# A third unit's split weights in places of their own, and the first feed-forward's pair in two other banks

## The chip, the cores and the metric

The kernel runs on one core of one Trainium2 chip. The metric is the device time of one execution in microseconds, the median of several executions. A trace of one further execution, with every instruction of every engine, was taken with the hardware profiler.

## What is computed

Two transformer-like blocks one behind the other, on one sequence of 512 tokens with 1024 features, all in float32:

```
x = first_block(x, c, ...)     # adaptive shift and scale from c; three mixers (S5, latent attention, gated spatial unit)
                               # merged by gates; layer norm; SwiGLU feed-forward; layer norm
h = second_block(x, ...)       # h += attention(rms(h)); h += swiglu(rms(h)); h += mlstm(rms(h)); h += swiglu(rms(h)); rms(h)

def swiglu(h, w_in, w_out):
    a, b = jnp.split(h @ w_in, 2, axis=-1)      # 1024 x 5632, hidden width 2816
    return (jax.nn.silu(a) * b) @ w_out
```

The attention of the second block has 8 heads in three groups of dilated windows (projection 1024 x 9216, output 1024 x 1024). The mLSTM has 8 heads (projection 1024 x 3088, output 1024 x 1024). There are three feed-forwards: number 0 in the first block, 1 and 2 in the second.

## The kernel before

Activations lie with the 128 features of a tile on the partitions and the 512 tokens along the free dimension; there are KD = 8 such tiles. Almost all of the time goes into multiplying them by weights that are used once. The weights are cut into units of 128 output columns (8 blocks of 128 x 128, and 11 in the feed-forwards' output). Each product is made in three matmuls so that it keeps float32 precision: activations are kept as a high and a low part (h_hi, h_lo), and so are the weights (w_hi, w_lo).

**The path of a unit.** SyncE loads it from memory into one of four raw tiles (N_RAW = 4). GpSimd splits it into w_hi (a pass that adds zero and rounds) and w_lo (a pass that subtracts), in `split_unit` and, inside loops, `split_at`; these go to one of two pairs of places (N_SPLIT = 2), by the unit's number modulo 2. TensorE uses them in `cols_mm` (24 matmuls of 512 columns for a unit of 8 blocks) or, tile by tile, in `tile_mm`. The semaphores count units: `units_split` up to where GpSimd is, `units_used` up to where TensorE is. GpSimd splits unit u only when unit u - 2 is used:

```
wait(pool, "units_used", u - N_SPLIT + 1)
```

All engines work through their instructions in order, and the order is written out by hand. The stages with their unit names are: w_mix_out, w_ff0_in_a, w_ff0_out_a, w_ff0_in_b, w_ff0_out_b, w_att (8 heads of 8 units), w_att_out, then the second feed-forward, w_ml, w_ml_out, and the third feed-forward. A feed-forward is done in two halves, a and b, of FFH = 11 hidden tiles with two units each: the gate and the other factor.

**The start of a stage.** The first two units of a stage are often worked on together (`pair_mm`, order `by_tile`), tile by tile, since the tiles of h_hi and h_lo come one after another from the norm in front of it. Both units are then in use up to the end, and unit 2 of the stage (the third) needs the place of unit 0. In the output projections of the attention and the mLSTM, units 0 and 1 are run over the finished heads while the last head is still being worked on (`last_head`, `last_heads`), and end with the last head's tile.

**First feed-forward.** The pair goes to the two banks g[0] and g[1]. ScalarE makes the tiles of h_hi (`norm_tiles`), then eight tiles of x, the residual (scaled and shifted from xn), then issues a DMA for the positions, and then enters the loop `one`: Silu of the gate bank to ff_s. VectorE multiplies it by the other bank and splits the product into u_hi and u_lo (`hidden`). TensorE's gate of the next hidden tile goes to the same bank, so it waits for the Silu (`gate_free`).

**Attention input.** The first head has its own order (`first_head`): the pair, then units 2 to 5 in the banks bc, ba, bb, bd. Behind unit 3 TensorE sums the rows of squares (`sum_rows`), for which VectorE adds up eight tiles of squares (`add_square`); ScalarE and VectorE make the inverse deviation of it (rstd), and VectorE scales the projections with it. TensorE's value projection (`project_values`) waits for the copies of five of them.

**Residual.** In an output projection VectorE adds each result to x (`tile`), and TensorE reuses a bank when the addition out of it is counted in `res_added`. The next stage's h_hi and h_lo and the squares are made in between.

Memory: the arena of 115 KB is shared by stage; `at(kb, ...)` places a tile at an offset in it. u_hi and u_lo lie at 0 and 22 KB, qk of the even heads at 44 KB, ml_qk at 0 KB.

Of the kernel before, what the change touches and what calls it, by code (L numbers as in the profile page):

```python
# [106 lines left out]
CONV_AT = [1] + [2 * n for n in range(1, 8)]  # L107
CONSTS = 2
# [22 lines left out]
def two_blocks(nc, t, out):  # L131

    ctx = ExitStack()
    with ctx:
# [112 lines left out]
        xn = at(46, "xn", [P, KD, SEQ])  # L247

# [192 lines left out]
        def _(pool):  # L441
# [23 lines left out]

            def low_part(u):
# [36 lines left out]
            for name, size, count in RUNS:  # L503
                u0 = FIRST[name]
                if name == "w_att":
                    with pool.Fori(0, 8) as h:
                        for s in range(8):
                            split_at(8 if s < 6 else 12, h, 8, u0 + s)
                    continue
                n = count // N_RAW  # L510
                if n > 1:
                    with pool.Fori(0, n) as i:
                        for s in range(N_RAW):
                            split_at(size, i, N_RAW, u0 + s)
# [7 lines left out]
        def _(pe):  # L522
# [96 lines left out]
            def residual(name, kb, xs, nth, shift=False, lead=None, **first):  # L619
# [5 lines left out]
                def pair(i):  # L625
                    for s in range(2):
                        ready(i * 2 + (u0 + s))
                        wait(pe, "res_added", i * 2 + (nth * 8 + s - 1))
                        cols_mm(g[(u0 + s) % 2], (u0 + s) % 2, kb, xs, **(first if isinstance(i, int) and s == 0 else {}))
                    if shift and isinstance(i, int):  # L630
                        first_tile()
                if lead is not None:
                    lead()
                    with pe.Fori(1, 4) as i:
# [4 lines left out]
            def feed_forward(n):  # L639
                for half, ab in enumerate("ab"):  # L640
# [17 lines left out]
                    else:  # L658
                        pe.wait_ge(S["res_added"], added - (n > 0))
                        pair_mm((bc, bd) if n else (first, second), u0, (h_hi, h_lo), H_SPLIT[f"ff{n}"] - 8,  # L660
                                late_tile if n else by_tile)
                        if n:
                            sum_rows(SQ[f"ff{n}"])
                            ready(u0 + 2)
                            cols_mm(first, u0 % 2, 8, (h_hi, h_lo))
                            ready(u0 + 3)
                            cols_mm(second, (u0 + 1) % 2, 8, (h_hi, h_lo))
                        with pe.Fori(2 if n else 1, FFH) as i:
# [327 lines left out]
            def first_head(s):  # L996
# [6 lines left out]
                cols_mm((bc, ba, bb, bd)[s - 2], (u0 + s) % 2, 8, (h_hi, h_lo))  # L1003
# [230 lines left out]
        def _(act):  # L1234
# [255 lines left out]
            def feed_forward(n):  # L1490
                for half, ab in enumerate("ab"):
                    u0 = FIRST[f"w_ff{n}_in_{ab}"]
                    j0 = (n * 2 + half) * FFH
                    def one(i):
                        wait(act, "units_used", i * 2 + (u0 + 1))
                        wait(act, "ff_mul", i + j0)
                        act.activation(ff_s[:], g[u0 % 2], ACT.Silu).then_inc(S["ff_silu"], 1)  # L1497
# [5 lines left out]
                    if n == 0:  # L1503
                        peeled(act, FFH, one)
                        if half == 0:
                            wait(act, "pos_phase", 1)
                            act.activation(rope_s[:], a0, ACT.Sin)
                            act.activation(rope_c[:], a1, ACT.Sin)
                            act.drain().then_inc(S["pos_trig"], 1)
                        continue  # L1510
# [6 lines left out]
            for k in range(KD):  # L1517
                act.activation(x[:, k, :], xn[:, k, :], ACT.Identity, scale=ln_cols[:, 2, k:k + 1], bias=ln_cols[:, 3, k:k + 1])
            act.drain()
# [1171 lines left out]
```

## Time and profile before

| | |
|---|---|
| median of 3 runs | 2638.06 us (2636.12 to 2644.28) |
| the profiled execution's own time | 2635.93 us |
| its span, first to last instruction | 2634.1 us |
| matmuls | 2481.6 us, 94% of the span |
| VectorE busy | 1489.8 us, 57% |
| GpSimd busy | 1647.6 us, 63% |
| ScalarE busy | 499.8 us, 19% |
| mean granted clock of TensorE | 0.962 of full speed |

A matmul's time in the trace includes its way through the array, and matmuls overlap; the step from one to the next is shorter than the duration shown. Times of day in the rows are microseconds from the span's start.

### The profile page before, as it was taken

The numbers are of one execution on the slowest core, as the hardware profiler recorded it, in microseconds if no ns is written. First come the engines' busy times: TensorE is split into PE (matmuls) and PEld (weight loads), VectorE is DVE, ScalarE is ACT, GpSimd is POOL, SyncE is SP. The second block draws the span as 40 slices with busy tenths as digits, with TensorE's granted clock in tenths as the row PEclk, the third lists the DMA queues.
The fourth block names the chain that finished last, engine by engine and source line by source line (L and its number), as shares of the span: only waits on it lengthen the run. The fifth ranks groups of instructions, "written<-read, shape, count | busy, mean of one in ns | idle before, by whom it ended". The sixth has DMA issues, their size and how long they took to land.

```text
span 2634.1 us, 33940 instructions
## 1 busy us (share of the span) xinstructions
PE 2481.6 (94%) x11937; PEld 2010.8 (76%) x11937; DVE 1489.8 (57%) x1796; ACT 499.8 (19%) x968; POOL 1647.6 (63%) x700
## 2 busy tenths in 40 slices
PE   6998999997999997999999989999999998999997
PEld 4776776775888875888888878888877666888886
DVE  5867334686464467754544455534588567544446
ACT  4533222103000004121211121000141442100000
POOL 4425445574777774655666557777777324787774
PEclk7999999997999998999999999999999989999998
DMA  6212333421332322222222223323322101332331
GB/s 244 71 55 81 123 149 121 152 77 53 96 104 88 102 90 68 77 76 84 77 84 78 81 61 96 113 78 96 112 74 88 48 27 51 92 107 84 96 107 53
DMA packets 61230, 237.70 MB, mean 90 GB/s; under 512 B 7072, under 2 KB 12200, under 8 KB 57424
## 3 DMA queue, kind: packets, MB, share of 16 engines
q1 hardware_dynamic: 54720, 230.51, 26.6%
q10 hardware_dynamic: 6416, 5.95, 0.7%
q8 instruction: 57, 0.93, 0.2%
q14 instruction: 37, 0.30, 0.0%
HBM read 232.24 MB, written 2.10 MB: 89 GB/s over the span
## 4 chain that ended last, share of the span: by engine, by line
PE 83%; DVE 8%; ACT 3%; issue 2%; DVEq 1%; ACTq 1%; POOL 1%; DMA 1%; POOLq 0%
PE gg L532 19%; PE gg L533 19%; PE gg L534 19%; PE babcd L570 2%; PE babcd L572 2%; PE babcd L571 2%; PE gg L906 2%; PE gg L908 1%; PE gg L907 1%; PE babcd L532 1%; PE babcd L533 1%; PE babcd L534 1%; PE babcd L1151 1%; PE be L882 1%; PE be L1177 1%
## 5 line engine op out<-in xcount | busy, mean ns | idle before, releaser
L462 POOL TENSOR_TENSOR w_hi<-raw,zero 128x1024 fp32r<-128x1024 f32 (+2 forms) x280 | 580.9, 2075 | 609.5 <-PE gg L534 386.0
L464 POOL TENSOR_TENSOR w_lo<-raw,w_hi 128x1024 fp32r<-128x1024 f32 (+2 forms) x280 | 748.5, 2673 | 39.9
L532 PE MATMUL gg<-h_hi,w_hi 128*128 128x512 f32 x1568 | 622.6, 397 | 14.4 <-ACT ff_s L1497 5.2
L533 PE MATMUL gg<-h_lo,w_hi 128*128 128x512 f32 x1568 | 617.4, 394 | 0.0
L534 PE MATMUL gg<-h_hi,w_lo 128*128 128x512 f32 x1568 | 616.6, 393 | 0.0
L532 PEld LDWEIGHTS gg<-h_hi,w_hi 128*128 128x128 f32 x1568 | 299.0, 191 | 85.5 <-issue 12.3
L534 PEld LDWEIGHTS gg<-h_hi,w_lo 128*128 128x128 f32 x1568 | 298.5, 190 | 63.4
L533 PEld LDWEIGHTS gg<-h_lo,w_hi 128*128 128x128 f32 x1568 | 298.9, 191 | 60.9
L2027 DVE TENSOR_TENSOR ta<-ff_s,gg 128x512 f32<-128x512 f32 x64 | 44.0, 688 | 331.1 <-PE gg L534 323.6
L453 POOL TENSOR_TENSOR w_hi<-raw,zero 128x1536 fp32r<-128x1536 f32 (+2 forms) x48 | 107.2, 2234 | 188.1 <-PE babcd L534 142.1
L532 PE MATMUL gg<-u_hi,w_hi 128*128 128x512 f32 x528 | 209.7, 397 | 4.2 <-issue 4.2
L533 PE MATMUL gg<-u_lo,w_hi 128*128 128x512 f32 x528 | 208.8, 395 | 0.0
L534 PE MATMUL gg<-u_hi,w_lo 128*128 128x512 f32 x528 | 208.8, 395 | 0.0
L1684 DVE TENSOR_TENSOR u_lo<-ta,u_hi 128x512 f32 (+1 forms) x66 | 178.5, 2704 | 9.3 <-issue 6.0
L455 POOL TENSOR_TENSOR w_lo<-raw,w_hi 128x1536 fp32r<-128x1536 f32 (+2 forms) x48 | 139.1, 2897 | 6.8
L570 PE MATMUL babcd<-w_hi,h_hi 128*128 128x384 f32 (+1 forms) x352 | 127.9, 363 | 9.3 <-ACT pt_res L1567 6.6
L1502 ACT ACTIVATE ff_s<-sq 128x512 f32<-128x512 f32 x44 | 27.9, 634 | 542.8 <-DVEq L2023 539.8
L571 PE MATMUL babcd<-w_hi,h_lo 128*128 128x384 f32 (+1 forms) x352 | 125.7, 357 | 0.0
L572 PE MATMUL babcd<-w_lo,h_hi 128*128 128x384 f32 (+1 forms) x352 | 125.7, 357 | 0.0
L532 PEld LDWEIGHTS gg<-u_hi,w_hi 128*128 128x128 f32 x528 | 99.2, 188 | 30.4 <-issue 6.8
L534 PEld LDWEIGHTS gg<-u_hi,w_lo 128*128 128x128 f32 x528 | 99.2, 188 | 24.0
L533 PEld LDWEIGHTS gg<-u_lo,w_hi 128*128 128x128 f32 x528 | 99.2, 188 | 24.0 <-issue 0.2
(568 smaller groups left out, 3893.0 us busy)
## 6 DMA issues: line engine op xcount, KB each, us to landing
raw<-in_w_ff_in_a SPq DMA_DIRECT2D x66, 512.0 KB, 3.5
raw<-in_w_ff_in_b SPq DMA_DIRECT2D x66, 512.0 KB, 3.5
raw<-in_w_att_qk SPq DMA_DIRECT2D x48, 512.0 KB, 3.6
raw<-in_w_ff_out_a SPq DMA_DIRECT2D x24, 704.0 KB, 4.1
raw<-in_w_ff_out_b SPq DMA_DIRECT2D x24, 704.0 KB, 4.1
late_raw<-in_w_ada SPq DMA_DIRECT2D x16, 1024.0 KB, 5.0
raw<-in_w_ml SPq DMA_DIRECT2D x25, 512.0 KB, 3.5
raw<-in_w_merge_a SPq DMA_DIRECT2D x16, 768.0 KB, 5.3
```

The source lines that it names most:

```text
L453: pool.tensor_tensor(hi, a, zero[:].to_broadcast([P, size * P]), ALU.add)
L455: pool.tensor_tensor(lo, a, hi, ALU.subtract).then_inc(S["units_split"], 1)
L462: pool.tensor_tensor(hi, a, zero[:].to_broadcast([P, size * P]), ALU.add)
L464: pool.tensor_tensor(lo, a, hi, ALU.subtract).then_inc(S["units_split"], 1)
L532: pe.matmul(dst, w_hi[slot][:, blk], xs[0][:, k, :], start=k == 0, stop=False)
L533: pe.matmul(dst, w_hi[slot][:, blk], xs[1][:, k, :], start=False, stop=False)
L534: mm = pe.matmul(dst, w_lo[slot][:, blk], xs[0][:, k, :], start=False, stop=k == kb - 1)
L570: pe.matmul(dst, xs[0][:, k, tok], w_hi[slot][:, blk], start=first and j == 0, stop=False)
L571: pe.matmul(dst, xs[1][:, k, tok], w_hi[slot][:, blk], start=False, stop=False)
L572: mm = pe.matmul(dst, xs[0][:, k, tok], w_lo[slot][:, blk], start=False, stop=last and j == len(ks) - 1)
L906: pe.matmul(g[m % 2], w_hi[slot][:, blk], h_hi[:, k, :], start=k == 0, stop=False)
L1684: v.tensor_tensor(lo, src, hi, ALU.subtract)
```

## The change

Unit 2 of four stages (w_ff0_in_a, w_att, w_att_out, w_ml_out) gets a pair of places of its own in the arena, `w_hi[2..5]` and `w_lo[2..5]`, found by `THIRD[name]`. GpSimd splits it with `split_third`, which waits not for a unit's use but for the former tenant of the place: the last unit of the stage before, or the scores of heads that lie there. TensorE reads it from there. The order of the splits and of the units stays. The loops of GpSimd and TensorE begin one round later, since the first is written out.

In the first feed-forward, half a, the pair goes to the banks bc and bd; units 2 and 3 go to g[0] and g[1], written out before the loop. Silu and `hidden` of the first hidden tile read bc and bd. The eight residual tiles and the DMA of the positions move on ScalarE from in front of the first Silu to behind it.

```diff
+THIRD = {"w_ff0_in_a": 2, "w_att": 3, "w_att_out": 4, "w_ml_out": 5}
...
+        for name, (hi_at, lo_at) in (("w_ff0_in_a", (18, 40)), ("w_att", (0, 4)), ("w_att_out", (44, 48)), ("w_ml_out", (0, 8))):
+            w_hi.append(at(hi_at, f"third_hi_{name}", [P, KD * P], F32R))
+            w_lo.append(at(lo_at, f"third_lo_{name}", [P, KD * P], F32R))
...
+            def split_third(name, tenant, done):
+
+                u, w = FIRST[name] + 2, THIRD[name]
+                pool.wait_ge(S[f"raw_landed{u % N_RAW}"], (u // N_RAW + 1) * 16)
+                pool.wait_ge(S[tenant], done)
+                a, hi, lo = raw[u % N_RAW][:, 0:KD * P], w_hi[w][:], w_lo[w][:]
+                pool.tensor_tensor(hi, a, zero[:, 0:1].to_broadcast([P, KD * P]), ALU.add)
+                pool.drain()
+                pool.tensor_tensor(lo, a, hi, ALU.subtract).then_inc(S["units_split"], 1)
...
+                if name in THIRD:
+                    for s in range(per):
+                        if s == 2:
+                            if name in ("w_ff0_in_a", "w_att"):
+                                split_third(name, "units_used", u0)
+                            elif name == "w_att_out":
+                                split_third(name, "att_scores", 14)
+                            else:
+                                split_third(name, "ml_scores", 4)
+                        else:
+                            split_unit(8 if s < 6 else 12, u0 + s, (u0 + s) % N_RAW, (u0 + s) % N_SPLIT)
...
-                        pair_mm((bc, bd) if n else (first, second), u0, (h_hi, h_lo), H_SPLIT[f"ff{n}"] - 8,
-                                late_tile if n else by_tile)
+                        pair_mm((bc, bd), u0, (h_hi, h_lo), H_SPLIT[f"ff{n}"] - 8, late_tile if n else by_tile)
                         if n:
                             sum_rows(SQ[f"ff{n}"])
-                            ready(u0 + 2)
-                            cols_mm(first, u0 % 2, 8, (h_hi, h_lo))
-                            ready(u0 + 3)
-                            cols_mm(second, (u0 + 1) % 2, 8, (h_hi, h_lo))
-                        with pe.Fori(2 if n else 1, FFH) as i:
+                        ready(u0 + 2)
+                        cols_mm(first, u0 % 2 if n else THIRD["w_ff0_in_a"], 8, (h_hi, h_lo))
+                        ready(u0 + 3)
+                        cols_mm(second, (u0 + 1) % 2, 8, (h_hi, h_lo))
+                        with pe.Fori(2, FFH) as i:
                             gate_up(i)
...
-                cols_mm((bc, ba, bb, bd)[s - 2], (u0 + s) % 2, 8, (h_hi, h_lo))
+                cols_mm((bc, ba, bb, bd)[s - 2], THIRD["w_att"] if s == 2 else (u0 + s) % 2, 8, (h_hi, h_lo))
...
                         if half == 0:
+                            one(0, bank=bc)
+                            for k in range(KD):
+                                act.activation(x[:, k, :], xn[:, k, :], ACT.Identity, scale=ln_cols[:, 2, k:k + 1], bias=ln_cols[:, 3, k:k + 1])
+                            act.drain()
+                            act.dma_start(pos_i[:], t["pos"].partition_broadcast(32)).then_inc(S["att_consts"], 16)
+                            with act.Fori(1, FFH) as i:
+                                one(i)
...
             norm_tiles(0, "ff0", xn)
-            for k in range(KD):
-                act.activation(x[:, k, :], xn[:, k, :], ACT.Identity, scale=ln_cols[:, 2, k:k + 1], bias=ln_cols[:, 3, k:k + 1])
-            act.drain()
-            act.dma_start(pos_i[:], t["pos"].partition_broadcast(32)).then_inc(S["att_consts"], 16)
             feed_forward(0)
```

In `residual`, the stages with a `lead` write out pair 1 (units 2 and 3), whose first unit reads `THIRD[name]`, and loop from 2.

## Rows read from the trace of the kernel before

**Rows 1.** The page: busy times, and the chain that ended last by engine.

```profile
PE 2481.6 (94%) x11937; PEld 2010.8 (76%) x11937; DVE 1489.8 (57%) x1796; ACT 499.8 (19%) x968; POOL 1647.6 (63%) x700
...
PE 83%; DVE 8%; ACT 3%; issue 2%; DVEq 1%; ACTq 1%; POOL 1%; DMA 1%; POOLq 0%
```

**Rows 2.** Two lines of VectorE: durations in ns (min/median/max), first and last start.

```profile
L2027 DVE TENSOR_TENSOR ta<-ff_s,gg x9: 686/687/690, 664.7 to 751.8; 128x512 f32<-128x512 f32 x9
...
L1966 DVE SCALAR_TENSOR_TENSOR x<-gg,one_col,x x6: 750/752/752, 1552.2 to 1580.2; 128x512 f32<-128x512 f32 x6
```

**Rows 3.** Timeline, first feed-forward: start, us, operation [idle before, its releaser].

```profile
607.85 2.08 PE L605 MATMUL bf<-ta,ones 128*128 128x512 f32 x2 [5.51 <-DVEq L1997]
...
632.42 5.75 ACT L1518 ACTIVATE x<-xn,ln_cols 128x512 f32<-128x512 f32 x8
...
634.89 1.89 POOL L462 TENSOR_TENSOR w_hi<-raw,zero 128x1024 fp32r<-128x1024 f32 x1 [27.78 <-PE gg L546]
...
636.93 2.35 POOL L464 TENSOR_TENSOR w_lo<-raw,w_hi 128x1024 fp32r<-128x1024 f32 x1
...
639.89 0.60 ACT L1497 ACTIVATE ff_s<-gg 128x512 f32<-128x512 f32 x1
...
640.63 0.76 PE L532 MATMUL gg<-h_hi,w_hi 128*128 128x512 f32 x1 [5.20 <-ACT ff_s L1497]
```

**Rows 4.** Attention input: the additions of squares together, then the timeline.

```profile
L1934 DVE TENSOR_TENSOR tb<-tb,sq x7: 691/2180/2692, 1031.5 to 1043.5; 128x512 f32<-128x512 f32 x7
...
1033.43 0.63 PE L532 MATMUL babcd<-h_hi,w_hi 128*128 128x512 f32 x1 [3.89 <-POOL w_lo L464]
...
1041.16 4.99 DVE L1934 TENSOR_TENSOR tb<-tb,sq 128x512 f32<-128x512 f32 x2 [0.51 <-ACT sq L1533]
...
1046.24 1.13 PE L592 MATMUL be<-tb,ones 128*128 128x512 f32 x2
...
1061.76 0.69 PE L570 MATMUL babcd<-w_hi,h_hi 128*128 128x384 f32 x1 [2.67 <-DVE qk L2300]
```

**Rows 5.** Timeline, start of the attention's output projection.

```profile
1539.09 0.75 DVE L1966 SCALAR_TENSOR_TENSOR x<-gg,one_col,x 128x512 f32<-128x512 f32 x1 [1.15 <-PE gg L546]
...
1543.98 0.79 PE L532 MATMUL gg<-o_hi,w_hi 128*128 128x512 f32 x1 [4.23 <-POOL w_lo L464]
...
1552.18 0.75 DVE L1966 SCALAR_TENSOR_TENSOR x<-gg,one_col,x 128x512 f32<-128x512 f32 x1 [5.75 <-PE gg L534]
```

**Rows 6.** Timeline, the mLSTM's last head and the start of its output projection.

```profile
2184.59 2.62 POOL L464 TENSOR_TENSOR w_lo<-raw,w_hi 128x1024 fp32r<-128x1024 f32 x1
2186.57 1.19 DVE L2509 SCALAR_TENSOR_TENSOR whole<-og,whole 128x512 f32<-128x512 f32 x1
...
2190.22 0.69 DVE L1704 TENSOR_TENSOR ta<-ta,em 128x512 f32<-128x512 f32 x1
...
2195.98 0.50 PE L544 MATMUL gg<-hd_hi,w_hi 128*128 128x512 f32 x1 [3.10 <-DVE hd_lo L2514]
...
2206.97 0.75 DVE L1966 SCALAR_TENSOR_TENSOR x<-gg,one_col,x 128x512 f32<-128x512 f32 x1 [1.05 <-PE gg L546]
...
2211.86 0.79 PE L532 MATMUL gg<-hd_hi,w_hi 128*128 128x512 f32 x1 [4.23 <-POOL w_lo L464]
...
2220.56 0.75 DVE L1966 SCALAR_TENSOR_TENSOR x<-gg,one_col,x 128x512 f32<-128x512 f32 x1 [6.25 <-PE gg L534]
```

**Rows 7.** Windows: busy us (instructions) of each engine, then granted clock, DMA share, GB/s.

```profile
640.60:644.50 3.90, 3.87 (x9) 3.12 (x10) 3.73 (x3) 0.00 (x0) 2.90 (x2) 0.50 0.33 126
...
1033.40:1037.10 3.70, 3.67 (x9) 2.88 (x10) 3.46 (x3) 2.33 (x5) 3.56 (x2) 0.54 0.58 213
...
1061.80:1067.60 5.80, 5.80 (x18) 5.80 (x19) 5.28 (x9) 0.00 (x0) 3.75 (x2) 0.50 0.17 52
...
2196.00:2199.00 3.00, 3.00 (x14) 2.45 (x14) 1.28 (x2) 0.63 (x1) 0.00 (x0) 1.00 0.02 5
```

**Rows 8.** Idle time ahead of L532's matmuls, 1586 to 1700, by releaser: us, times.

```profile
  POOL w_lo L464: 0.5, 1
```

More of the change, by code:

```diff
@@ L504, in _ @@
                 u0 = FIRST[name]
+                per = 8 if name == "w_att" else N_RAW
+                if name in THIRD:
[9 more added lines that the diff above has]
+                            split_unit(8 if s < 6 else 12, u0 + s, (u0 + s) % N_RAW, (u0 + s) % N_SPLIT)
                 if name == "w_att":
-                    with pool.Fori(0, 8) as h:
+                    with pool.Fori(1, 8) as h:
                         for s in range(8):
@@ L511, in _ @@
                 if n > 1:
-                    with pool.Fori(0, n) as i:
+                    with pool.Fori(int(name in THIRD), n) as i:
                         for s in range(N_RAW):
@@ L628, in pair @@
                         wait(pe, "res_added", i * 2 + (nth * 8 + s - 1))
-                        cols_mm(g[(u0 + s) % 2], (u0 + s) % 2, kb, xs, **(first if isinstance(i, int) and s == 0 else {}))
+                        third = lead is not None and isinstance(i, int) and s == 0
+                        cols_mm(g[(u0 + s) % 2], THIRD[name] if third else (u0 + s) % 2, kb, xs, **(first if isinstance(i, int) and s == 0 else {}))
                     if shift and isinstance(i, int):
@@ L633, in residual @@
                     lead()
-                    with pe.Fori(1, 4) as i:
+                    pair(1)
+                    with pe.Fori(2, 4) as i:
                         pair(i)
@@ L1493, in feed_forward, with one @@
                     j0 = (n * 2 + half) * FFH
-                    def one(i):
+                    def one(i, bank=g[u0 % 2]):
                         wait(act, "units_used", i * 2 + (u0 + 1))
                         wait(act, "ff_mul", i + j0)
-                        act.activation(ff_s[:], g[u0 % 2], ACT.Silu).then_inc(S["ff_silu"], 1)
+                        act.activation(ff_s[:], bank, ACT.Silu).then_inc(S["ff_silu"], 1)
                     def scaled(i):
@@ L1509, in feed_forward @@
                             act.drain().then_inc(S["pos_trig"], 1)
+                        else:
+                            peeled(act, FFH, one)
                         continue
@@ L2033, in scaled_hidden @@
                         hidden(i)
-                    if n == 0:
+                    if n == 0 and half == 0:
+                        hidden(0, bank=bd)
+                        with v.Fori(1, FFH) as i:
+                            hidden(i)
+                    elif n == 0:
                         peeled(v, FFH, hidden)
```

1 line of the change is left out of this document (removed).

## Prediction

> **What bounds the kernel now.** The page comes first: TensorE's matmuls cover 94% of the span and 83% of the chain that ended last, GpSimd is busy 63% and VectorE 57% [rows 1]. So only what stands between two matmuls, or makes matmuls slow, is worth anything. The list of what TensorE waited for shows where it stands still; at each of these places the timeline gives the wait, and the view of windows the clock that was granted behind it. In steady work a weight unit (24 matmuls) takes 5.44 us in the feed-forward inputs (nine products 87.1 us apart over eight pairs of units: 87.1 / 16) and 5.60 us in the output projections (28.0 / 5) [rows 2]. GpSimd needs 1.89 + 2.35 us for its two passes over a unit, up to 2.62 us for the second where VectorE works beside it [rows 3, 6], so it keeps pace. It falls behind only at a stage's start, where units 0 and 1 finish almost together and the split of unit 2 could not begin before.
>
> Four such places are touched. Each early split waits for the former tenant of its place, and every later split stands behind it on GpSimd, which works in order; the tenants (the last unit of the stage before, seven heads' scores, four heads' scores) are done long before GpSimd gets there, so this wait costs nothing. First feed-forward: TensorE idles 5.20 us up to 640.63; here the split was done at 639.28, and the release is the Silu at 639.89, behind the eight residual tiles (5.75 us) [rows 3]. Attention input: 3.89 us up to 1033.43 [rows 4]. Attention output: 4.23 us up to 1543.98 [rows 5]. mLSTM output: a gap of the same kind up to 2211.86 [rows 6]. Behind these gaps the clock is 0.50 to 0.54, the lower of its two levels (1.2 GHz), for about 4 to 6 us; a matmul then takes 3.9 / 9 = 0.43 us instead of 5.44 / 24 = 0.227 [rows 2, 7].
>
> **First feed-forward.** After the change the pair goes to two other banks, so unit 2 needs neither the Silu nor the residual tiles; its split can run from 607 on, while GpSimd had nothing to do for 27.78 us [rows 3]. TensorE leaves the pair at 640.63 - 5.20 = 635.43 and goes on. Unit 3 is split from about 635.5 to 640.2 (1.89 + 0.15 + 2.62); TensorE wants it at 635.43 + 5.44 = 640.87, so the wait is nothing, with only 0.7 us to spare. Units 2 to 5 then end at 635.43 + 4 x 5.44 = 657.2, and the product that read the last of them at 664.7 [rows 2] starts at 657.3: 7.4 us won (5.2 of gap, the rest matmuls at the lower clock). The moved work: the table load and Silu end about 636.7, the eight tiles take 5.75 us, the position DMA's issue about 0.4, so ScalarE is at the second Silu near 643 and done by 644. TensorE asks for it with unit 4, at 646.3; 2 us of cover. Were that gone, each us of ScalarE would cost one.
>
> **Attention output.** Unit 2 is now released by the first residual addition (1539.09 + 0.75 = 1539.84, matmul about 1540.0) and ends at 1545.6; the addition behind it moves from 1552.18 to 1545.7 [rows 5]. 6.5 us won. Its early split follows unit 1's directly, beside the last head's scores, which VectorE reads from PSUM; at worst it holds up a tiny product by 0.5 us, under matmuls. I take nothing. The first additions shift against GpSimd's passes; a unit later they are back in step, since TensorE needs tile k's addition only at unit k + 2; I take nothing and keep 1 us for the range.
>
> **mLSTM output.** The same sum: first addition done 2206.97 + 0.75 = 2207.72, unit 2 from 2207.9 to 2213.5, next addition at 2213.6 instead of 2220.56: 7.0 us [rows 6]. But the early split starts when GpSimd is free, at 2184.59 + 2.62 = 2187.2, and its second pass lasts from about 2189.25 to 2191.6. In that time falls VectorE's maximum of two SBUF tiles at 2190.22 (0.69 us alone), on the chain to the last head's output. Rows tell what such a meeting does: the product of two SBUF tiles at 2186.57 took 1.19 us, ending 0.55 after GpSimd's pass (2187.21) [rows 6]; the sums of two SBUF tiles took 0.69 us alone, and 2.18 at the median, 2.69 at most, beside it [rows 4]. So the maximum ends at 2192.15 rather than 2190.91: 1.24 us lost, between 0 (no meeting) and 2. This lengthens TensorE's idle stretch before 2195.98 from 3.10 to 4.34 us. Behind 3.10 the clock was still 1.00; behind 3.89 and 4.23 it was down [rows 4, 5, 6, 7]. 4.34 lies beyond those, so I take the lower clock for the 12 matmuls ahead of the last square sums: 12 x 0.20 = 2.4 us more lost (0 is the other end). Net 7.0 - 1.2 - 2.4 = 3.4 us, between 3.4 and 7.0.
>
> The Trainium skill, page "SBUF — State Buffer", section "Who interferes with whom", says that a VectorE operation with two SBUF inputs and a GpSimd operation that reads SBUF take one shared port pair in turn, the later one standing still until the first is done. By it the early splits are not free although GpSimd was idle; 2190.22 would be held, as the rows at 2186.57 bear out. Without the rule and its rows the sum would be 3.6 us better here.
>
> **Attention input.** Unit 2 would run from 1029.54 to 1035.0 and unit 3 to 1040.4 instead of 1046, 5.7 us earlier. What is late next is the column-sum of squares behind unit 3: it waits for VectorE's last addition, which ended at 1041.16 + 4.99 = 1046.15, and the matmul came at 1046.24 [rows 4]. Until now the two were level. VectorE's seven additions are long because of GpSimd, and replaying them against the new splits (unit 3's 1029.7 to 1034.4, unit 4's 1035.15 to 40.3, unit 5's 1040.6 to 45.3), an addition ending 0.55 us behind a pass that it meets, gives 1046.6: 0.4 us later than before. TensorE idles 6 us, so the sum of rows runs at the lower clock: 2.08 us, as the same shape did at 607.85 [rows 3], against 1.13: 0.95 more. All of VectorE's chain behind it moves by 1.35 us, and with it the copy that released the value projection at 1061.76 [rows 4]; units 4 and 5 are covered by that chain, with about 1 us left. But TensorE's idle time there shrinks from 2.67 us towards 1 us, so the clock may hold; before, 18 matmuls in 5.8 us ran at 0.50 [rows 7], 0.32 us each against 0.174 later in the same unit (half of it, plus the small extra that the 512-column rows show: 0.227 for 0.213). That returns 18 x 0.146 = 2.6 us. Net 1.2 us won; ends: 1.4 lost (clock low again), 5.7 won (squares not held up).
>
> **Sum.** 7.4 + 6.5 + 3.4 + 1.2 = 18.5 us. The profiled execution took 2635.93 us around its 2634.1 span, so 2617.4; the median shown is 2638.06, 2.1 above it. From the median: 2619.5 us.
>
> The Trainium skill, page "TensorE: Matmul & The Clock Gate", section "Wait — 56ns, not 53.3ns?", gives 215.7 ns between starts of 512-column matmuls at the full clock. A unit would be 5.18 us by it, and the sum about 1.1 us better (estimate: 0.26 x 1 + 0.42 x 2). The rows show 227 and 233 ns here, so the trace does not agree and decides.
>
> **Rivals.**
> - Nothing late next (10%): no meeting of GpSimd and VectorE matters, every gap closes in full: 7.4 + 5.7 + 6.5 + 7.0 = 26.6, 2611.5 us. For it: GpSimd has only 63% busy. Against: additions of 2.18 us at the median [rows 4].
> - Part is given back (17%): the loops' first rounds are now written out, and unit 3, split last, comes late; 0.7 us of spare at the first stage is thin. With 1 us lost at each of three stages and the attention input at its bad end: 7.4 + 6.5 + 3.4 - 1.4 - 3.0 = 12.9, 2625.2 us. Against: in the middle feed-forward, whose units 2 and 3 are written out already, the wait for a split is 0.5 us in all [rows 8].
> - It does not do what it says (5%): GpSimd, strictly in order, reaches the third split no earlier. Then only the moved Silu helps, until the split's end at 639.28: 1.2 us, 2636.9. Against: 27.78 us idle [rows 3], and tenants that are long done.
> - Slower (3%): the new 6 us of idle time in the attention input leaves the clock low far into the first head. At 0.20 us a matmul it must last over 18.5 / 0.20 = 92 matmuls to undo the gain, and 132 to show 0.3% slower (2646). The rows show the return after 4 to 6 us each time, some 9 to 18 matmuls [rows 7].
>
> **Numbers.** The likeliest case (65%) is 18.5 won; its own range is 2615 to 2624. The range takes in the "nothing late" end and the giving back: 2611.5 to 2627. A difference under 0.3% (7.9 us) can't be told from none. All of the first three cases are faster by more: 92%; same 5%, slower 3%.
>
> **What would show it.** In the changed trace no idle time between the first pair and unit 2 in the first feed-forward, at most 0.5 us in both output projections; the eight residual tiles behind the first Silu. In the attention input a wait of about 6 us in front of the sum of rows instead of 3.89 in front of unit 2. In the mLSTM's last head a maximum of near 2 us instead of 0.69, and a granted clock of 0.5 for the unit behind it. The prediction is wrong if the squares end by 1043 (more won), or if TensorE waits for unit 3's split, or for the second Silu.

## The result and the profile after

The changed kernel takes 2620.85 us (median of 4 runs, 2614.89 to 2622.95); the kernel before, on the same chip, 2641.17 us (4 runs, 2636.12 to 2645.22). The ratio is 0.9919, 95% interval 0.9901 to 0.9937: 21.4 us won, with 16.6 and 26.1 as the ends (2641.17 x 0.0081, x 0.0063, x 0.0099); the two medians differ by 20.3 us. The whole interval lies beyond the 0.3% that the prediction takes as the least difference to be told from none. The profiled execution took 2622.95 us around a span of 2620.9, at a mean granted clock of 0.964.

The page, busy times and the chain that ended last; they hardly differ from [rows 1], because what went away was idle time between matmuls:

```profile
PE 2480.9 (95%) x11937; PEld 2007.9 (77%) x11937; DVE 1488.6 (57%) x1796; ACT 499.2 (19%) x968; POOL 1647.5 (63%) x700
...
PE 84%; DVE 8%; ACT 2%; issue 2%; DVEq 1%; ACTq 1%; DMA 1%; POOL 1%; POOLq 0%
```

**First feed-forward**, timeline of the changed kernel (start, us, operation, idle time before it and its releaser):

```profile
606.83 2.34 POOL L477 TENSOR_TENSOR third_hi_w_ff_in_a<-raw,zero 128x1024 fp32r<-128x1024 f32 x1
609.31 2.35 POOL L479 TENSOR_TENSOR third_lo_w_ff_in_a<-raw,third_hi_w_ff_in_a 128x1024 fp32r<-128x1024 f32 x1
...
634.53 0.60 ACT L1525 ACTIVATE ff_s<-babcd 128x512 f32<-128x512 f32 x1 [1.10 <-PE babcd L573]
635.02 5.75 ACT L1535 ACTIVATE x<-xn,ln_cols 128x512 f32<-128x512 f32 x8
...
635.33 1.90 POOL L458 TENSOR_TENSOR w_hi<-raw,zero 128x1024 fp32r<-128x1024 f32 x1 [23.68 <-PE babcd L573]
...
637.37 2.42 POOL L460 TENSOR_TENSOR w_lo<-raw,w_hi 128x1024 fp32r<-128x1024 f32 x1
...
641.46 0.60 ACT L1525 ACTIVATE ff_s<-gg 128x512 f32<-128x512 f32 x1 [0.69 <-PE gg L561]
```

The split of unit 2 runs in time that GpSimd idled away before [rows 3], the residual tiles stand behind the first Silu, and the second Silu waits for TensorE, not TensorE for it. Unit 3's split ends at 639.79 (637.37 + 2.42), before TensorE needs it. No matmul between the pair and unit 2 has an idle time in front.

**Attention input**: the additions of squares, the sum of rows behind unit 3, and the first matmul of the value projection.

```profile
1024.59 14.47 DVE L1966 TENSOR_TENSOR tb<-tb,sq 128x512 f32<-128x512 f32 x7
...
1039.14 2.07 PE L619 MATMUL be<-tb,ones 128*128 128x512 f32 x2 [5.93 <-DVEq L1967]
...
1055.59 0.44 PE L597 MATMUL babcd<-w_hi,h_hi 128*128 128x384 f32 x1 [1.43 <-DVE qk L2336]
```

The wait of 3.89 us in front of unit 2 [rows 4] has become one of 5.93 in front of the sum of rows; TensorE was early and VectorE's additions were not: seven in 14.47 us, 2.07 on the mean, two of them 0.69 us and the other five 2.18 to 2.70.

**Attention output.** The wait of 4.23 us [rows 5] is 0.24, and the third addition (the second one shown) begins 6.67 us behind the first, where [rows 5] have 13.09:

```profile
1528.18 0.75 DVE L1998 SCALAR_TENSOR_TENSOR x<-gg,one_col,x 128x512 f32<-128x512 f32 x1 [1.15 <-PE gg L573]
1529.08 0.47 PE L559 MATMUL gg<-o_hi,third_hi_w_att_out 128*128 128x512 f32 x1 [0.24 <-DVE x L1998]
...
1534.85 0.75 DVE L1998 SCALAR_TENSOR_TENSOR x<-gg,one_col,x 128x512 f32<-128x512 f32 x1
```

**mLSTM output.** The early split's second pass and VectorE's maximum of two SBUF tiles lie beside each other, and the maximum takes 1.92 us where [rows 6] have 0.69:

```profile
2179.90 2.40 POOL L479 TENSOR_TENSOR third_lo_w_ml_out<-raw,third_hi_w_ml_out 128x1024 fp32r<-128x1024 f32 x1
...
2180.92 1.92 DVE L1736 TENSOR_TENSOR ta<-ta,em 128x512 f32<-128x512 f32 x1
...
2187.92 0.79 PE L571 MATMUL gg<-hd_hi,w_hi 128*128 128x512 f32 x1 [4.33 <-DVE hd_lo L2550]
...
2201.64 0.75 DVE L1998 SCALAR_TENSOR_TENSOR x<-gg,one_col,x 128x512 f32<-128x512 f32 x1 [1.06 <-PE gg L573]
2202.54 0.47 PE L559 MATMUL gg<-hd_hi,third_hi_w_ml_out 128*128 128x512 f32 x1 [0.25 <-DVE x L1998]
...
2208.28 0.75 DVE L1998 SCALAR_TENSOR_TENSOR x<-gg,one_col,x 128x512 f32<-128x512 f32 x1
```

The windows, with the same columns as [rows 7]: behind the first pair, behind the sum of rows, from the value projection on, behind the last head's wait, and at unit 2 of the mLSTM output.

```profile
635.60:641.00 5.40, 5.40 (x25) 4.36 (x24) 4.56 (x3) 5.17 (x8) 4.12 (x3) 1.00 0.05 5
1039.10:1042.00 2.90, 2.85 (x5) 1.63 (x6) 0.03 (x1) 0.69 (x1) 0.00 (x0) 0.50 0.60 181
1055.60:1061.40 5.80, 5.80 (x33) 5.80 (x34) 5.26 (x9) 0.00 (x0) 5.04 (x2) 1.00 0.30 90
2188.00:2193.40 5.40, 5.40 (x14) 4.24 (x14) 1.21 (x2) 0.63 (x1) 0.00 (x0) 0.50 0.00 0
2202.50:2208.20 5.70, 5.66 (x25) 4.73 (x26) 4.90 (x4) 2.42 (x4) 4.51 (x2) 1.00 0.00 0
```

The clock is full where a gap was closed (1.00 where [rows 7] have 0.50 behind 640.6), low behind the new wait of the sum of rows, full again at the value projection, and low behind the longer wait of the last head.

**Where the time went.** The span is cut at instructions that every kernel here has. Stretch A runs from the sum of rows of the layer norm (607.85 in [rows 3]) to the product of the third hidden tile; B from the pair's first matmul of the attention input to the first addition of the attention output; C from there to the third addition; E from the start of the last head's maximum in the mLSTM to the third addition of its output. Both kernels were traced twice; us:

| stretch | before | before, second trace | after | after, second trace | won, mean |
|---|---|---|---|---|---|
| A first feed-forward | 56.89 | 56.93 | 49.74 | 49.80 | 7.14 |
| B attention | 523.17 | 523.19 | 519.67 | 519.64 | 3.5 |
| C attention output | 13.09 | 13.09 | 6.67 | 6.67 | 6.4 |
| E mLSTM output | 30.34 | 30.65 | 27.36 | 26.60 | 3.5 |
| between A and B | 351.18 | 351.19 | 351.17 | 351.18 | 0 |
| between C and E (second feed-forward, mLSTM heads) | 638.04 | 646.08 | 646.07 | 638.13 | 0 |
| span | 2634.1 | 2641.0 | 2620.9 | 2614.5 | |

A + B + C + E make 20.6 us, beside 21.4 by the ratio. The stretch between C and E takes 638 or 646 us in either kernel; that is why the first two traces differ by only 13.2 us and the second two by 26.5. What is "won" in this table is not yet what the edits did: the experiments show B's 3.5 us without any early split.

### The profile page after: what moved, and what is told of

Read it like the earlier page. It is cut to its first block, busy times and chain, and to the rows that moved or that the text cites. A ratio compares the mean times of both kernels' runs of the same rounds, so it can differ in the third digit from the quotient of the medians.

```text
span 2620.9 us, 33849 instructions
## 1 busy us (share of the span) xinstructions
PE 2480.9 (95%) x11937; PEld 2007.9 (77%) x11937; DVE 1488.6 (57%) x1796; ACT 499.2 (19%) x968; POOL 1647.5 (63%) x700
## 4 chain that ended last, share of the span: by engine, by line
PE 84%; DVE 8%; ACT 2%; issue 2%; DVEq 1%; ACTq 1%; DMA 1%; POOL 1%; POOLq 0%
PE gg L559 19%; PE gg L560 19%; PE gg L561 19%; PE babcd L597 2%; PE babcd L599 2%; PE babcd L598 2%; PE gg L934 2%; PE gg L936 1%; PE gg L935 1%; PE babcd L559 1%; PE babcd L560 1%; PE babcd L561 1%; PE babcd L1179 1%; PE be L910 1%; PE be L1205 1%
## 5 line engine op out<-in xcount | busy, mean ns | idle before, releaser
L467 POOL TENSOR_TENSOR w_hi<-raw,zero 128x1024 fp32r<-128x1024 f32 (+2 forms) x260 | 540.5, 2079 | 453.1 <-PE gg L561 348.2
L469 POOL TENSOR_TENSOR w_lo<-raw,w_hi 128x1024 fp32r<-128x1024 f32 (+2 forms) x260 | 695.3, 2674 | 37.7 <-issue 1.3
L458 POOL TENSOR_TENSOR w_hi<-raw,zero 128x1024 fp32r<-128x1024 f32 (+2 forms) x64 | 139.8, 2184 | 332.1 <-PE babcd L561 153.7
L561 PEld LDWEIGHTS gg<-h_hi,w_lo 128*128 128x128 f32 x1560 | 297.8, 191 | 63.2
L460 POOL TENSOR_TENSOR w_lo<-raw,w_hi 128x1024 fp32r<-128x1024 f32 (+2 forms) x64 | 181.9, 2843 | 9.1
```

The costliest lines, as they stand in the source:

```text
L458: pool.tensor_tensor(hi, a, zero[:].to_broadcast([P, size * P]), ALU.add)
L460: pool.tensor_tensor(lo, a, hi, ALU.subtract).then_inc(S["units_split"], 1)
L467: pool.tensor_tensor(hi, a, zero[:].to_broadcast([P, size * P]), ALU.add)
L469: pool.tensor_tensor(lo, a, hi, ALU.subtract).then_inc(S["units_split"], 1)
L561: mm = pe.matmul(dst, w_lo[slot][:, blk], xs[0][:, k, :], start=False, stop=k == kb - 1)
```

## The experiments

Unless a diff is said to be against the kernel before, it is against the changed kernel. The column "stages" of the table at the end of this section is A + B + C + E, against the means of the two traces of before (56.91, 523.18, 13.09, 30.50).

**The stages one by one.** `KEEP` names the stages whose unit 2 has a place of its own; the others go back to the two shared ones. The banks, the moved tiles and the written-out first rounds stay in all of them.

```diff
-                        if s == 2:
+                        if s == 2 and name in KEEP:
...
-                cols_mm((bc, ba, bb, bd)[s - 2], THIRD["w_att"] if s == 2 else (u0 + s) % 2, 8, (h_hi, h_lo))
+                cols_mm((bc, ba, bb, bd)[s - 2], THIRD["w_att"] if s == 2 and "w_att" in KEEP else (u0 + s) % 2, 8, (h_hi, h_lo))
```

`KEEP = ("w_ff0_in_a",)`, only the first feed-forward:

> Only the first feed-forward keeps its early third split, its other banks and the moved tiles; the other three stages split unit 2 as before, though their first rounds stay written out. Theory (each stage by itself): 7.4 us less than before, and the gaps of 3.9, 4.2 and 4.2 us in front of unit 2 come back in the attention input and the two output projections. Rival (written-out rounds or early splits cost something elsewhere, or the gain is made up later): clearly less than 7 us at the value that VectorE's product of the third hidden tile starts, counted from the stage's first matmul.

Measured: 2629.6 us (6 runs) against 2643.24, ratio 0.9955 (0.9940 to 0.9970). A is 49.74, C 13.23 and E 30.54: the first feed-forward's gain is all there, and the outputs are as before. B is 519.73 with the attention input's code as before, 3.4 us shorter than in both traces of before. So B's 3.5 us don't need the attention input's early split; the kernel with no early split at all, further down, has 519.84.

`KEEP` without `"w_att"`:

> The changed kernel without the early split of the attention input. Theory (the sum of squares is late next, and only the clock behind it wins something): the gap of 3.9 us comes back in front of unit 2, the wait of 5.9 us in front of the sum of rows goes, the sum of rows takes 1.13 us again instead of 2.07, and the first value matmul comes 1.2 us earlier than in the changed kernel, counted from the pair's first matmul (45.9 instead of 47.1 us); the clock behind it is the lower one again and costs 2 to 3 us, so the whole is 0 to 3 us slower than the changed kernel. Rival (the early split is worth its full unit): 5.7 us slower than the changed kernel.

Measured: 2620.9 us (4 runs), ratio 0.9925 (0.9903 to 0.9947), which is the changed kernel's 0.9919. The sum of rows comes 30.32 us behind the pair's first matmul (30.63 with the early split), the value projection 45.84 (47.08), B is 519.76 (519.67). The early split of the attention input is worth 0.1 us: 1.24 us lost up to the value projection, and about as much won behind it.

`KEEP` without `"w_ml_out"`:

> The changed kernel without the early split of the mLSTM output. Theory (the early split holds up the maximum of the last head, and the longer idle time lowers the clock): the maximum takes 0.69 us again instead of 1.92, the idle time in front of head 6's last part is 3.1 us instead of 4.3, the clock behind it stays at 1.00, and the gap of 4.2 us in front of unit 2 comes back; from the maximum's start to the third addition 30.3 us instead of 27.4, so about 3 us slower than the changed kernel. Rival (the early split costs nothing there): 7 us slower, and the maximum as it is in the changed kernel.

Measured: 2623.86 us (4 runs), ratio 0.9929 (0.9907 to 0.9950). The maximum takes 0.69 us again and E is 30.33, as before; that part's 3 to 4 us are lost. The expected clock of 1.00 didn't come: behind the wait of 3.10 us the first matmul takes 0.79 us, as at the low clock. B is 523.53 in this trace although the instructions up to there are those of the changed kernel: that stretch has two lengths in either version. 1.6 of the 3.9 us lie at the value projection. In the changed kernel all its first matmuls run at the full clock; here the clock falls after the first seven, in the midst of dense work:

```profile
1057.42 0.33 PE L598 MATMUL babcd<-w_hi,h_hi 128*128 128x384 f32 x1
1057.59 0.43 PE L599 MATMUL babcd<-w_hi,h_lo 128*128 128x384 f32 x1
1057.82 0.53 PE L600 MATMUL babcd<-w_lo,h_hi 128*128 128x384 f32 x1
...
1060.70 0.53 PE L600 MATMUL babcd<-w_lo,h_hi 128*128 128x384 f32 x1
1061.02 0.39 PE L598 MATMUL babcd<-w_hi,h_hi 128*128 128x384 f32 x1
```

In the kernel of the first feed-forward alone, whose wait there is that of [rows 4] (2.68 against 2.67 us), the low clock ends with the ninth matmul; in both traces of the kernel before 18 were slow:

```profile
1053.49 0.69 PE L598 MATMUL babcd<-w_hi,h_hi 128*128 128x384 f32 x1 [2.68 <-DVE qk L2337]
...
1055.90 0.52 PE L599 MATMUL babcd<-w_hi,h_lo 128*128 128x384 f32 x1
1056.21 0.46 PE L600 MATMUL babcd<-w_lo,h_hi 128*128 128x384 f32 x1
1056.52 0.34 PE L598 MATMUL babcd<-w_hi,h_hi 128*128 128x384 f32 x1
```

The other 2.1 to 2.2 us of B lie in the first two heads: from the copy of the first head's values to that of the second it takes 65.4 us in both traces of before and in this one, and 63.2 to 63.3 in the others, save 64.7 with the banks alone. Behind a wait of 2.4 us that all have near the head's end, the low clock lasts longer in the first group.

**The third split ahead of unit 1's in the mLSTM output**, so that it is over before the maximum. The semaphore still counts units in order: the third split doesn't count, and unit 1's split counts two.

```diff
-                            else:
-                                split_third(name, "ml_scores", 4)
+                        elif name == "w_ml_out" and s == 1:
+                            split_third(name, "ml_scores", 4, count=0)
+                            split_unit(8, u0 + 1, (u0 + 1) % N_RAW, (u0 + 1) % N_SPLIT, count=2)
```

> The changed kernel with the mLSTM output's unit 2 split ahead of unit 1, in GpSimd's idle time before the last gate unit is used. Theory: the split no longer meets the maximum, which takes 0.69 us again; idle time 3.1 us, clock 1.00, no gap in front of unit 2: from the maximum's start to the third addition about 23.4 us instead of 27.4, 3.6 us faster than the changed kernel. Rival 1 (it isn't the meeting): the maximum stays near 1.9 us. Rival 2 (the clock drops whatever the gap): maximum short, but the 12 matmuls behind it at the lower clock, and only 1.2 us won.

Measured: 2617.95 us (4 runs), ratio 0.9910 (0.9887 to 0.9934). The third split now begins 24 us ahead of the maximum, which is back to 0.69 us, and the wait behind it to 3.11:

```profile
2154.89 1.88 POOL L477 TENSOR_TENSOR third_hi_w_ml_out<-raw,zero 128x1024 fp32r<-128x1024 f32 x1
2156.91 2.34 POOL L479 TENSOR_TENSOR third_lo_w_ml_out<-raw,third_hi_w_ml_out 128x1024 fp32r<-128x1024 f32 x1
...
2178.74 0.69 DVE L1739 TENSOR_TENSOR ta<-ta,em 128x512 f32<-128x512 f32 x1
```

```profile
2184.50 0.57 PE L574 MATMUL gg<-hd_hi,w_hi 128*128 128x512 f32 x1 [3.11 <-DVE hd_lo L2553]
```

E is 24.97 instead of 27.36, 2.4 us more won; against the changed kernel's second trace (26.60) it is 1.6. 3.6 us were expected. From the maximum to the first addition it still takes 18.30 us, against 16.75 in the first trace of before: the clock fell behind 3.11 us too, so this part of the expected gain was not all to be had.

**The squares in PSUM banks.** In the attention input ScalarE writes the tiles of squares to two free banks, and VectorE's additions have one operand there instead of two in SBUF. The expectation and its rival name two causes for the late sum of rows.

```diff
-                act.activation(sq[k % 2][:], x[:, k, :], ACT.Square).then_inc(S["sq_ready"], 1)
+                act.activation((bf, be)[k % 2][:], x[:, k, :], ACT.Square).then_inc(S["sq_ready"], 1)
...
+                from_ = (bf, be) if nth == SQ["att"] else sq
...
-                    v.tensor_tensor(tb[:], tb[:], sq[k % 2][:], ALU.add)
+                    v.tensor_tensor(tb[:], tb[:], from_[k % 2][:], ALU.add)
```

> The changed kernel; the eight squares of the attention's norm go to two PSUM banks instead of two SBUF tiles, so that VectorE's additions have one SBUF input only and need not take turns with GpSimd. Theory (GpSimd's passes are what makes the sum of squares late): each of the 7 additions takes 0.7 to 0.8 us instead of 2.2, the sum of rows comes right behind unit 3, about 25 us after the pair's first matmul instead of 30.6, and the first value matmul after about 40.5 us instead of 47.1; the clock is low again behind the idle 2.7 us there, so 4 to 5.5 us faster than the changed kernel. Rival (the chain of ScalarE's squares is what bounds): the additions short, but the sum of rows not before 29 us.

Measured: 2613.71 us (4 runs) against 2637.04 (13 runs), ratio 0.9915 (0.9893 to 0.9937). Every addition takes 0.69 us, five of the seven in the midst of GpSimd's passes, and the last ends at 1034.36; the sum of rows comes 24.79 us behind the pair's first matmul, the value projection 40.30 (45.84 before, 47.08 after), at the full clock although TensorE had idled 2.66 us:

```profile
1031.05 2.40 POOL L460 TENSOR_TENSOR w_lo<-raw,w_hi 128x1024 fp32r<-128x1024 f32 x1
...
1032.26 0.69 DVE L1967 TENSOR_TENSOR tb<-tb,bf 128x512 f32<-128x512 f32 x1 [0.72 <-ACT bf L1565]
...
1033.67 0.69 DVE L1967 TENSOR_TENSOR tb<-tb,be 128x512 f32<-128x512 f32 x1 [0.72 <-ACT be L1565]
```

```profile
1034.44 1.12 PE L619 MATMUL be<-tb,ones 128*128 128x512 f32 x2
...
1049.95 0.45 PE L597 MATMUL babcd<-w_hi,h_hi 128*128 128x384 f32 x1 [2.66 <-DVE qk L2337]
```

B is 512.80, 6.9 us under the changed kernel. That is more than the 4 to 5.5 us expected, since the expectation had the low clock behind this wait. The ratio can't tell this kernel from the changed one, the stretch can. The Trainium skill, page "SBUF — State Buffer", section "Who interferes with whom", says that a VectorE instruction with at most one SBUF input, outside the modes that use two ports, doesn't contend with GpSimd; 0.69 us here, beside 2.07 on the mean with two, agrees.

The counterpart, squares in PSUM but the attention input's unit 2 back in the shared place:

> The changed kernel with the squares in PSUM banks and without the third place for the attention input. Theory (both the late additions and the late split have to go, either alone brings nothing): unit 2 stands again about 3.9 us behind the pair, the sum of rows comes about 30.2 to 30.4 us after the pair's first matmul, bounded by unit 3 and no longer by the additions (0.69 us each), and the first value matmul 45.8 us or a little less; the time is that of the kernel without the attention input's third place, 2621 us, that is about 6 us above the squares in PSUM with the third place. Rival (the squares alone were the limit, the early split adds nothing): the sum of rows at about 25 us and the value matmul at about 40.3, the time 2614.

Measured: 2618.07 us (6 runs) against 2642.77 (11 runs), ratio 0.9915 (0.9898 to 0.9932). Unit 2 is late again and the additions are not:

```profile
1026.54 0.50 PE L560 MATMUL babcd<-h_hi,w_hi 128*128 128x512 f32 x1 [3.89 <-POOL w_lo L461]
...
1039.18 1.02 PE L620 MATMUL be<-tb,ones 128*128 128x512 f32 x2
...
1054.60 0.69 PE L598 MATMUL babcd<-w_hi,h_hi 128*128 128x384 f32 x1 [2.71 <-DVE qk L2338]
```

With this the four cases are complete. Us from the pair's first matmul to the value projection, and B:

| | squares in SBUF | squares in PSUM |
|---|---|---|
| unit 2 in the shared place | 45.84, 519.8 | 45.57, 519.6 |
| unit 2 in its own place | 47.08, 519.7 | 40.30, 512.8 |

Either edit alone wins at most 0.3 us at the value projection; together they win 5.5 there and 7.0 in B. About 1.4 of the 7.0 is the clock, full behind the wait of 2.66 us in this kernel and low for about nine matmuls behind the 2.68 and 2.71 us of the upper row.

**Both of these edits** (squares in PSUM, third split ahead of unit 1's in the mLSTM output), twice:

> The squares through PSUM and the mLSTM output's third split ahead of unit 1, together. Theory: the two are independent, 4 to 5.5 us and 2.4 us less than the changed kernel, 2612 to 2615 us. Rival (one takes the other's gain, or the clock takes it back): no faster than the better of the two.

> The kernel with squares in PSUM banks and the third split ahead of unit 1's at the mLSTM output once more, with more rounds. Theory: ratio to the kernel before 0.988 to 0.990, about 13 us under the changed kernel's 2621 less what chance in the mLSTM heads does, 2607 to 2611 us; the value matmul 40.3 us behind the pair, the third addition to x 23.4 to 25.0 us behind the last maximum of 0.69 us. Rival (the gain seen once was mostly chance of the clock in the mLSTM heads): 2613 or more.

Measured: 2607.66 us (4 runs) against 2637.04, ratio 0.9888 (0.9870 to 0.9906); and 2610.82 us (5 runs) against 2642.77, ratio 0.9890 (0.9871 to 0.9908). B is 512.8 and 512.9, E 23.41 and 23.42. The first time lies below the 2612 to 2615 us expected, the second within its 2607 to 2611. Behind the last head's wait the clock stays up here, which makes E 1.6 us shorter than in the kernel with the split ahead of unit 1's alone:

```profile
2171.85 0.50 PE L574 MATMUL gg<-hd_hi,w_hi 128*128 128x512 f32 x1 [3.10 <-DVE hd_lo L2554]
2172.18 0.40 PE L575 MATMUL gg<-hd_lo,w_hi 128*128 128x512 f32 x1
```

By the stages this kernel is 10.4 us faster than the changed one, and it is the fastest here.

**Filling the wait.** If the low clock behind the last head's wait comes of its 4.33 us of idle time, eight needless matmuls in it should keep the clock. They are of 512 columns and stand in front of the part that waits.

```diff
-                unit(0, 4, 6)
+                unit(0, 4, 5)
+                for n in range(8):
+                    pe.matmul(bd, w_hi[u0 % 2][:, 0:P], h_hi[:, 0, :], start=True, stop=True)
+                unit(0, 5, 6)
```

> The changed kernel with 8 needless matmuls of 512 columns into a bank that nobody reads, in the middle of the last head's idle stretch (the output is the same). Theory (idle time lowers the clock, and the 12 matmuls behind it pay): the idle time in front of head 6's last part falls from 4.3 to 2.4 us, the clock behind it is 1.00, 12 matmuls take 2.8 instead of 5.2 us; the maximum still takes 1.9 us; from its start to the first addition about 18.3 us instead of 20.7. Rival (the clock there goes by something else, as the three low ones behind 3.1 us suggest): still low, nothing won.

Measured, in one execution of 2619.21 us: the eight matmuls take 2.00 us straight behind the part before, from 2179.94 on, and the idle time behind them is 2.95, longer than expected because the maximum took 2.39 us in this trace. The filler so shortens the wait and doesn't break it up. The clock is low all the same (0.80 us for the first matmul), for seven matmuls:

```profile
2177.43 2.39 DVE L1739 TENSOR_TENSOR ta<-ta,em 128x512 f32<-128x512 f32 x1
```

```profile
2184.89 0.80 PE L571 MATMUL gg<-hd_hi,w_hi 128*128 128x512 f32 x1 [2.95 <-DVE hd_lo L2553]
```

From the maximum to the first addition it takes 19.96 us instead of 20.72, but the second trace of the changed kernel has 19.95 without the filler. The filler won nothing that can be seen. Whether idle time is what lowers the clock it doesn't decide: 2.95 us of it were left, and behind 3.1 us the clock falls in some traces and not in others.

**Only the banks and the moved tiles** (`KEEP = ()`):

> The other banks, the moved residual tiles and the written-out rounds alone; no unit has places of its own. Theory (in the first feed-forward both the Silu and the split were late, the split 1.2 us less): unit 2 there starts about 1.2 us earlier than in the kernel before, with the lower clock behind it as before, released by GpSimd's second pass; the other three stages as before; 1 to 2 us less than before in all. Rival (the moved tiles and banks alone carry the 7.1 us of that stage): product of the third hidden tile 49.7 us after the norm's matmul instead of 55.7.

Measured: 2637.44 us (10 runs) against 2637.04 (13 runs), ratio 0.9994 (0.9982 to 1.0005). A is 56.30, 0.6 us better than before. Unit 2 starts 31.54 us behind the norm's sum of rows, 1.24 us earlier than before (32.78), as expected; but 12 of its matmuls run at the low clock instead of nine, which takes back 0.6. TensorE now waits for the split instead of the Silu, 3.91 us instead of 5.20:

```profile
640.69 0.79 PE L560 MATMUL gg<-h_hi,w_hi 128*128 128x512 f32 x1 [3.91 <-POOL w_lo L461]
```

Of the 7.15 us of the first feed-forward, 6.6 come of the early split on top of the other banks. The early split with the old banks was not run. By [rows 3] it would have won about nothing alone (an estimate): the Silu that frees the bank ends at 640.49 (639.89 + 0.60), behind the end of the late split at 639.28. Here too, then, two edits may be worth much together and little alone.

**Both kernels traced once more**, to see which stretches repeat:

> The kernel before, unchanged, traced a second time. Theory (what the parts of the change don't account for is chance of the clock in the heads, not an effect of the change): the stretches that the change touches repeat within 0.1 us: 56.9 us from the row of the layer norm to the third product of the first feed-forward, 30.3 from the pair to the sum of rows, 13.1 to 13.3 from the first to the third addition of the attention output; but the time from the first value matmul to the attention output's first addition, 477.3 in the first trace, comes at 474 or at 477, and the time from there to the mLSTM's last maximum, 638.0 in the first trace, anywhere from 638 to 647. Rival (the first trace is typical of the kernel before, and the change shortens or lengthens the heads): 477 and 638 again.

> The changed kernel, unchanged, traced a second time. Theory (chance in the heads): 49.7 us to the third product, 30.6 to the sum of rows, 6.7 between the first and the third addition of the attention output again; the time from the third addition to the mLSTM's last maximum, 646.1 in the first trace, anywhere from 638 to 647, and the last maximum either 0.7 (it falls beside GpSimd's pass) or 1.9 to 2.4 us. Rival (the changed kernel's heads are slower by themselves): 646 again.

Measured: the table at the head of this document's result. A and C repeat within 0.1 us. The stretch between C and E swaps its 638 and 646 us, so neither length belongs to one of the kernels (the other kernels have 638.1 to 646.5 there); the expectation that B would vary in the kernel before is not borne out by these two (523.17 and 523.19), only by kernels with the same code there (519.8). The last head's maximum took 2.37 us in the second trace of the changed kernel.

| kernel | stages, us won | by the ratio, us won (interval) |
|---|---|---|
| changed kernel | 20.6 | 21.4 (16.6 to 26.1) |
| first feed-forward alone | 10.4 | 11.9 (7.9 to 15.9) |
| without the attention input | 20.4 | 19.8 (14.0 to 25.6) |
| without the mLSTM output | 13.4 | 18.8 (13.2 to 24.6) |
| third split ahead of unit 1's | 22.6 | 23.8 (17.4 to 29.9) |
| squares in PSUM | 27.1 | 22.4 (16.6 to 28.2) |
| squares in PSUM, no third place there | 21.1 | 22.5 (18.0 to 27.0) |
| both edits | 31.1, again 30.9 | 29.5 (24.8 to 34.3), again 29.1 (24.3 to 34.1) |
| banks and tiles alone | 3.6 | 1.6 (-1.3 to 4.7) |

All the values by stages lie within the intervals. The stages tell kernels apart that the ratios don't.

## Why the prediction was right

2619.5 us was forecast and 2620.85 measured; 18.5 us were forecast, against 20.6 by the traces' stages and 21.4 by the ratio. The mechanism held in the first feed-forward and the attention output, in the mLSTM output but for one reason, and in the attention input but for the size of one term. That the number came so near is in part luck: the attention input's term was 1.1 us too large, and 3.4 us of clock that the sum doesn't have came on top. Step by step:

- **First feed-forward, 7.4:** 7.15. No idle time, unit 3's split in time, the second Silu not waited for.
- **Attention output, 6.5:** 6.4.
- **mLSTM output, 3.4** (7.0 less 1.2 less 2.4): 2.98 between the first traces, 4.05 between the second. The meeting of GpSimd's pass and the maximum is there: 1.23 us lost in the first trace (1.92 for 0.69) and 1.68 in the second. The clock term, 2.4 us, measured 2.74 between the first traces (3.97 us more from the maximum to the first addition, less 1.23) and nothing between the second (1.64, less 1.68). It was reasoned wrongly in one half. That the clock falls behind 4.34 us held, in all five traces with a wait of 4.33 to 4.78 us there. That it survives 3.10 did not hold in general: behind 3.1 us it stayed up to the first addition in three of eight traces (16.7 us from the maximum to the first addition: before, and both edits twice) and fell in five (18.2 to 18.3 us). In the kernel before, what is lost ahead of the first addition is won back behind it, which keeps the size of the whole term near: it took 16.75 + 13.59 in one trace and 18.31 + 12.34 in the other.
- **Attention input, 1.2:** 0.1. Two of its three terms held. The additions' end moved the sum of rows by 0.31 us (0.4 forecast), and the sum of rows took 2.07 for 1.13 us. The value projection was 1.24 us late (1.35). The term that was mis-sized is the clock given back there, 2.6 us, from 18 slow matmuls in the one trace at hand. The kernels with that wait and the other traces' clock have nine slow ones, so 1.3 us was to be had (9 x 0.146), and the first head's copies of v confirm it: 16.95 us behind the first value matmul in the changed kernel, 18.3 without its early split, 19.7 in both traces of before. 1.3 pays for 1.24. Against the traces of before alone the forecast of this stage would have looked right; the kernel without the early split shows that half of those 2.8 us (19.7 to 16.95) come without it.
- **What the sum left out:** 3.4 us in B that both traces of before have and most other kernels have not, whatever their code there. It is the granted clock at two places of the first two heads, the value projection (1.4 us) and behind the wait of 2.4 us (2.1 us). What decides when it returns was not found, nor whether these 3.4 us are chance.

With B's edit at 0.1, the four edits make 7.14 + 0.1 + 6.4 + 3.5 = 17.1 us. As far as the traces tell, the remaining 4 us of the ratio's 21.4 are that clock (3.4) and noise.

**The rivals.** "Nothing late next" (26.6 us) failed at the two meetings it denied; the kernel with both edits, in which these are taken away, won 31. "Part is given back" failed in the three stages from which it took 1 us each (7.1, 6.4 and 3.5 us won), and the attention input's 0.1 lies above its bad end of 1.4 lost. "It does not do what it says" is refuted by the split at 606.83. "Slower" needed 92 matmuls at the low clock; the windows have 1.00 at the value projection.

## What to carry to other kernels

When a gap on the path is closed, look for what was level with it: here the squares stood 0.1 us from being the limit, and an edit at either alone was worth nothing, while both together were worth 7 us, 5.5 of them at that place. Put one operand of a VectorE operation into PSUM, or move GpSimd's pass, where the two would meet on the path; that made 2.07 us (on the mean) into 0.69 and 1.92 into 0.69. And cut the span at fixed instructions: A, B and C repeat within 0.1 us where whole runs scatter by 8. Trace a kernel more than once all the same, since E differed by up to 0.8 us between two traces of one kernel and B has two lengths for the same code.

## What the runs showed of the hardware

The granted clock doesn't follow from the length of the wait in front alone. Behind 3.1 us it was 1.00 in some traces and 0.50 in others; behind 2.67 us eighteen slow matmuls in one kernel and nine in another, with the same instructions; behind 1.59 us full for seven matmuls and then low for ten; behind 2.66 us not low at all. The two traces of before agree in B within 0.02 us, and the two of the changed kernel within 0.03, while the attention code of before has 519.8 in other kernels; between C and E two executions of one kernel differ by 8 us. No rule for it comes out of these runs. The Trainium skill, page "TensorE: Matmul & The Clock Gate", section "What's actually happening", says that the hardware's watch runs free of the kernel's start; a clock that falls in the midst of dense matmuls, as at 1057.82, fits that, but no run here tests it.

In the mLSTM's heads this makes a difference of 8 us between two executions of one kernel (638.0 and 646.1): up to the first head's maximum all traces take 517.8 to 518.2 us, and the granted clock of the stretch is 0.97 and 0.98 in the short ones and 0.96 in the long ones. The less than one percent that a change of this kind is worth must be read from stretches outside such places.
